# Where SP loads the indexer's key pages: one block ahead of the first layer's experts, or eight pages behind each of eight experts' weights

## The reference

```
layer 0: RMSNorm -> projection -> causal convolution mixer and forgetting attention -> output projection -> residual
         RMSNorm -> mixture of 16 experts (top group of 4, top 2 experts in it) -> residual
layer 1: RMSNorm -> projection -> sparse attention: an indexer scores all visible keys,
         each query keeps the best and attends to them -> output projection -> residual
         RMSNorm -> mixture of 16 experts -> residual; final RMSNorm
indexer: score[q, k] = sum over h of relu(q_idx[q, h] . k_idx[k] / 8) * w_idx[q, h]
```

## Time and profile before

| what | us |
|---|---|
| median of 3 runs | 1640.16 (1635.81 to 1641.26) |
| profiled execution, its own time | 1629.98 |
| its span | 1628.2 |
| TensorE busy | 1389.5 (85%) |
| key pages issued by SP | 390.83 to 471.61 |
| layer 0, output projection and router on TensorE | 391.56 to 469.16 |
| layer 0, experts on TensorE, from the first gather's arrival | 492.22 to about 794.5 |
| first index matmul on the key pages | after 854.58 |

### The profile page before, as it was taken

The page is one execution under the profiler, slowest core; times in us unless marked ns, Lnnn a source line. Parts: engine busy times, 40 slices in busy tenths (PEclk is TensorE's granted clock), DMA queues, the critical chain, the costliest instruction groups (busy, mean ns, idle before and its releaser), DMA issues.

```text
span 1628.2 us, 28717 instructions
## 1 busy us (share of the span) xinstructions
PE 1389.5 (85%) x11123; PEld 787.1 (48%) x11124; DVE 645.3 (40%) x1541; ACT 300.5 (18%) x773; POOL 145.7 (9%) x370
## 2 busy tenths in 40 slices
PE   7999668888958999989589987888999699998990
PEld 4444434444445554655254443455545455555650
DVE  2059944332143311111265899566412432111104
ACT  2110024332010000000111211445521000000002
POOL 0059100000000000000200000000000000000002
PEclk9999678999978999999889999799999699999995
DMA  8440127778154899999811021233332487999965
GB/s 268 173 169 1 58 67 230 226 231 297 47 201 161 326 368 368 399 398 416 309 38 52 1 100 61 76 105 105 105 155 98 141 309 286 396 386 390 404 272 197
DMA packets 86635, 341.60 MB, mean 210 GB/s; under 512 B 24791, under 2 KB 32055, under 8 KB 72534
## 3 DMA queue, kind: packets, MB, share of 16 engines
q1 hardware_dynamic: 66302, 289.80, 48.4%
q0 software_dynamic: 10656, 37.56, 6.8%
q10 hardware_dynamic: 9536, 12.33, 2.2%
HBM read 309.53 MB, written 30.47 MB: 209 GB/s over the span
## 4 chain that ended last, share of the span: by engine, by line
PE 55%; DVE 20%; DMA 10%; SPq 7%; issue 5%; ACT 2%; POOL 1%; ACTq 0%; DVEq 0%; POOLq 0%
PE banks L1098 18%; PE banks L1126 9%; PE banks L1027 7%; DVE arena L2148 6%; DMA arena<-in_wstream 6%; PE banks L796 4%; DVE arena L1665 4%; SPq L446 3%; PE banks L827 3%; DVE arena L1793 2%; SPq L472 2%; PE banks L946 2%; DMA arena<-hn_scratch,arena 2%; DVE arena L1787 1%; SPq L477 1%
## 5 line engine op out<-in xcount | busy, mean ns | idle before, releaser
L1098 PE MATMUL banks<-arena 128*32 128x128 f32 (+1 forms) x4736 | 363.3, 337 | 28.1 <-issue 17.3
L1098 PEld LDWEIGHTS banks<-arena 128*32 128x32 f32 (+1 forms) x4736 | 241.5, 127 | 148.4 <-issue 59.2
L1126 PE MATMUL banks<-arena 128*64 128x512 f32 (+1 forms) x1184 | 175.8, 503 | 1.1 <-ACT arena L1551 1.1
L1665 DVE TENSOR_TENSOR arena<-arena,banks 128x256 f32<-128x256 f32 (+5 forms) x84 | 38.9, 464 | 295.4 <-PE banks L1098 171.0
L796 PE MATMUL banks<-arena 128*128 128x512 f32 x320 | 139.9, 595 | 1.0 <-DMA arena<-in_wstream 0.9
L2042 DVE COPY arena<-banks 128x256 f32<-128x256 f32 (+1 forms) x56 | 21.4, 382 | 289.7 <-PE banks L1111 283.3
L1665 DVE TENSOR_TENSOR arena<-banks,arena 128x512 f32<-128x512 f32 (+5 forms) x159 | 70.6, 474 | 141.1 <-ACT arena L1475 86.6
L1665 DVE TENSOR_TENSOR arena<-arena 128x256 f32<-128x256 f32 (+17 forms) x248 | 98.7, 431 | 57.6 <-ACT arena L1416 36.1
L827 PE MATMUL banks<-arena 128*128 128x512 f32 x256 | 118.1, 607 | 0.0
L1027 PE MATMUL banks<-arena 128*128 128x512 f32 x256 | 111.2, 594 | 1.4 <-issue 0.8
L2148 DVE SCALAR_TENSOR_TENSOR arena<-arena 128x512 f32<-128x512 f32 x120 | 105.2, 937 | 1.1
(11 more groups left out here) (269 smaller groups left out, 1493.8 us busy)
## 6 DMA issues: line engine op xcount, KB each, us to landing
arena<-in_wstream SPq DMA_DIRECT2D x109, 2048.0 KB, 16.0
arena<-in_fox_kt SPq DMA_DIRECT2D x64, 256.0 KB, 2.9
arena<-in_fox_v SPq DMA_DIRECT2D x64, 256.0 KB, 3.0
arena<-in_dsa_page SPq DMA_DIRECT2D x64, 256.0 KB, 2.9
expert_rows<-arena ACTq DMA_DIRECT2D x76, 128.0 KB, 8.9
expert_rows<-arena POOLq DMA_DIRECT2D x1, 6656.0 KB, 20.2
hn_scratch<-arena POOLq DMA_DIRECT2D x8, 512.0 KB, 3.0
expert_rows<-arena ACTq DMA_DIRECT2D x72, 32.0 KB, 8.5
```

Of the source, the lines that this page charges most:

```text
L1098: last = mm(bank(b, 0, 4 * n, n * j, n * j + n), x[:, c, :], w[:, c, 4 * n * j:4 * n * j + 4 * n], start=(c == 0), stop=(c == DC - 1))
L1126: last = mm(bank(3, 0, 8 * n, n * q, n * q + n), ht2[g % 2][:, 128 * i + n * j:128 * i + n * j + n], w[:, c, 8 * n * q:8 * n * q + 8 * n], ...
L1665: return v.tensor_tensor(out, x, y, op)
```

## The change

The function `index_keys(n0, n1)` issues the pages n0 to n1-1 with the same instructions as before. The block of 64 goes; `experts(0)` calls the function behind the down load of each of the experts 2 to 9, with eight pages each: pages 0 to 7 behind expert 2, 56 to 63 behind expert 9. `experts(1)` issues none.

```diff
         first_weights(0, 1, 1)
-        for s in range(NS):
-            for j in range(NPG):
+
+        def index_keys(n0, n1):
+            for n in range(n0, n1):
+                s, j = divmod(n, NPG)
                 sp.dma_start(g3(k_idx[s // 2][64 * (s % 2):64 * (s % 2) + 64, :], NPG)[:, j, :],
                              page_rows(a["kidx_t"], page_id(s, j)))\
                     .then_inc(S("kidx"), 16)
...
                     weights(l, s, i, a["wstream"][bass.ds(k + (b + i), 1)].rearrange("a p w -> (a p) w"))
+                if l == 0 and s < 10:
+                    index_keys(8 * s - 16, 8 * s - 8)
```

## The result

The changed kernel takes 1643.91 us in the median of 20 runs (1635.76 to 1654.27), the kernel before 1632.12 us (1623.87 to 1646.82, 20 runs). The ratio is 1.0062, with a 95% interval of 1.0040 to 1.0083: slower by 10 us, and by 6.5 us at the least. The three runs shown before the prediction were from the upper part of what the kernel before does.

What follows compares the result with a forecast made beforehand. The chain that ended last was put at 55% TensorE and 10% DMA of the span, with large weight loads. A cost of 9.6 us less a lead of 5.8 gave +3.8 on the 1640.2 us median: 1644.0 us, range 1633 to 1651.

Steps and rivals of the forecast that it cites:

- 12.02 - 4.38 = 7.6 us: First layer's first expert gather: without the burst of three loads it takes the second layer's time, gaining 7.6 us.
- The step that took 1.8 us off again: Third expert's small gather: it comes late as in the second layer, cutting the lead from 7.6 to 5.8 us.
- The rival in which the gather is not helped: First gather: its 12.02 us have another reason, so only the cost stays: +9.6, 1649.8 us; chance 0.10.
- Expert 5: Its gate load goes out at 586.7, lands at 595.1, wanted at 597.75: no wait, but stream 4.5 us late.
- Expert 6: TensorE waits 6.5 us at the gate, runs a cold block, waits for the up load; 3.8 us lost.
- Experts 7 and 8: Worked out the same way: their loads come just ahead of their use; errors there counted to the second rival.
- the 5.8 us that I gave to experts 9 to 11: First layer's late experts: the delay grows from 3.8 us to 9.6 us at expert 11's gate load and stays.
- The cost of the pages' traffic: Pages on SP's queue among the expert loads: 0.12 us of the 16 engines a page, 1.0 us for eight.
- My 9.6 us: Total cost in the first layer's experts: expert 9's gate load 8.6 us late plus 1.0 us for the last pages.
- the second rival: More stalls at experts 8 and 10 from slower page issue: cost about 15 us, +9, 1649 us; chance 0.28.
- Cover holds: SP's 10.1 us pass unnoticed by TensorE: cost 2 us, lead 5.8, so -3.8, 1636.4 us; chance 0.20.
- some 8 as a sign of my forecast: TensorE's waits for weights in the first layer's experts grow in sum by about 8 us if the forecast is right.

Runs made afterwards that it cites:

- SP's time hidden: The change with its eight pages behind the up loads of experts 2 to 9 instead of the down loads; 1.0019 of the kernel before.
- wide rows: Against the kernel before: pages in SP's gaps ahead of the experts, plus one 256 KB DMA of 4 KB rows behind up loads 2 to 9; ratio 1.0009.
- the register loads: Against the kernel before: pages in SP's gaps ahead of the experts, plus 18 unused register loads on SP behind down loads 2 to 9; ratio 1.0022.
- the split: Against the kernel before: all 64 key pages moved into SP's gaps ahead of and between the first expert loads, none later in the stage; ratio 0.9963.
- the first early run: Against the kernel before: 32 pages in SP's gaps ahead of the experts, 32 behind the up loads of experts 2, 3 and 4; ratio 0.9895.
- the late half: Against the kernel before: 32 pages in SP's gaps ahead of the experts, 32 behind the up loads of experts 5, 7, 8 and 9; ratio 0.9976.

## Why the prediction was off, point by point

**The direction of the parts held, the net was too small.** I said +3.8 us on the profile and 1644.0 us, in a range of 1633 to 1651. The time fell at 1643.91, but that closeness is luck: it owes to the high median of the first three runs, which I had added to. As a ratio I said 1.0023 and it is 1.0062. "Same" was given 0.52 and "slower" 0.36; slower it is.

**The gather.** 12.02 - 4.38 = 7.6 us was right: 4.34 us, and the head shrinks by 7.4. The step that took 1.8 us off again, because the second layer's extra rows came late, was wrong for this profile: it read one wait of one profile as a property. In the runs here this wait varies from none to 3.2 us in the first layer. The rival in which the gather is not helped fell: behind three weight loads the gather took 9.61 us again. With it fell my use of the rule of the Trainium skill ("DMA: Bandwidth & Descriptors", section "Queues, rings and completion order"), that each engine goes round the queues with work: it does not follow from it that a gather goes past such a burst unharmed.

**Experts 2 and 3** had more cover than I wrote: 537 + 8.4 is 19.5 us ahead of 564.88, not 15. Nothing hangs on it.

**Expert 5** went as worked out: gate load out 11.4 us behind the down load (571.76 to 583.15), 8.5 us to land, no wait at the gate block at 594.05. The 0.31 us at 598.35 are a wait for its up load.

**Expert 6**: forecast a wait of 6.5 us at the gate, a cold block, and a second wait; measured 8.72, a block of 4.97, and none.

**Experts 7 and 8** are the step that failed. I had their loads "just ahead of their use", and no loss there. Expert 7 did not wait, but expert 8 waited 2.58 and 2.47 us. Its gate load went out at 638.9 and took 14.8 us. Counted from expert 2's down block, the changed kernel was 5.1 us late behind expert 6 (forecast 3.8), 10.5 late at expert 9's gate (forecast still 3.8), 16.2 late at expert 11's (forecast 9.6) and 14.9 at the end. So the 5.8 us that I gave to experts 9 to 11 came true, at 5.7, and nearly all of what is missing was lost at expert 8.

**The cost of the pages' traffic** was the term that was mis-sized. I took 1.0 us for eight pages from a stretch in which the engines were nearly idle, and counted it twice. That is 2.0 us, where all eight blocks come to some 7.5 by the same row. The runs show 15.6 us for all 64 with SP's time hidden (14.7 in wide rows; 8 to 9 by the timed ratios). And I had the issue time as the main term and the traffic as an addition to it; by the tails they cost 10.3 and 15.6 us alone and 17.0 together. My 9.6 us, of which 8.6 stood for the first delays and 1.0 for the last pages, are near what the register loads alone cost. The measured total, 14.9 against before, is that of the second rival (15), but by another mechanism: a page took 1.2 us on SP as before (9.49 us for eight), not the 1.4 and more that this rival asked for.

**Cover holds**, the first rival, did not: TensorE's waits for weights grew by 13.7 us, where I had named some 8 as a sign of my forecast.

**The rule of the Trainium skill** ("DMA: Bandwidth & Descriptors", section "Issuing engines are not separate DMA queues"), that the time to initiate a DMA is usually small beside the DMA: the run with the register loads speaks against relying on it here. They are not the issue itself, but SP's time for addresses in front of it, and cost 10.3 us of tail with no DMA of their own. But I had used the row against it to look past the traffic, and that was no less wrong.

Open: why a MB on SP's queue takes 5 to 7% longer when 2 MB of pages stand among the weights, whatever their row size; whether SP's time and the traffic add; and whether POOL's queue would avoid the cost.

## What to carry to other kernels

A move has two ends. Where the loads leave is one question (here a burst stood ahead of a gather that TensorE waited for, 7.4 us), where they go is another, and the best answer, gaps between waits ahead of the stage, kept the gain without the cost: 0.9963 and, with half of the pages behind early experts, 0.9953. Price added traffic in the stretch where it will run: 32 pages cost nothing measurable behind the early experts and some 12 us behind the late ones. And two delays of the same load need not add up; test each alone and both together.

## What was not expected of the hardware

- 2 MB of traffic in a backlogged stream cost 15.6 us of a 260 us stretch, in 512 rows a block or in 64 wide ones (14.7 us), by the tails, against 0.12 us for a 32 KB page in an idle stretch, some 7.5 us for 64.
- The wait for a 128 KB gather of 32 rows varied from 0 to 3.2 us in the first layer between runs in which its surroundings did not change.
- Waits of 2.58 and 2.47 us were followed by blocks of 3.67 us, as warm ones; waits of 2.87, 7.32 and 8.72 us by blocks of 5.32, 5.80 and 4.97. The restart is not paid at each wait. It also differed at one and the same block, the first of the tail: 5.35 us behind waits of 1.30 and 1.23 us for the extra rows (the split, the first early run), 3.65 us behind 1.39 and 1.26 us (pages behind the up loads, the late half).
